# A decoder layer with convolution, retention and experts: another order at the start, products of ones, and small work moved between engines

## The reference

```python
z = rmsnorm(x, norm1_g) @ w_in                   # 1024 x 3072
a, b, q, k, v, g = split(z)                      # six parts of 512 columns
u = a * sigmoid(b)                               # convolution group: depthwise, 31 taps
c = silu(layernorm(causal_depthwise_conv(u)))
q, k = rope(q), rope(k)                          # retention group: 4 heads of 128
o, state = retention(q, k, v)                    # chunks of 128 tokens, one after the other
o = silu(g) * group_norm(o)                      # norm of each head
x = x + concat(c, o) @ w_out
x = x + moe(rmsnorm(x, norm2_g))                 # 32 experts, 2 for each token, 1024 x 256
x = x + rmsnorm(p @ w_ple) * sigmoid(x @ w_ple_gate)
y = rmsnorm(x, final_norm_g)                     # the states are outputs too
```

## Time and profile before

| what | value |
| --- | --- |
| median of 3 runs | 738.96 us (735.79 to 739.05) |
| profiled execution | 741.15 us, span 739.4 us |
| mean granted TensorE clock | 0.97 |
| TensorE, VectorE, ScalarE, GpSimd busy | 685.8, 557.8, 405.3, 331.6 us |
| opening and convolution, to the first retention scores | about 0 to 176 us |
| retention and output projection | about 176 to 302 us |
| routing | about 302 to 337 us |
| experts | about 337 to 659 us |
| last stage | about 659 to 739 us |

### The profile page before, as it was taken

The page is one execution under the profiler, slowest core; times in us unless marked ns, Lnnn a source line. Parts: engine busy times, 40 slices in busy tenths (PEclk is TensorE's granted clock), DMA queues, the critical chain, the costliest instruction groups (busy, mean ns, idle before and its releaser), DMA issues.

```text
span 739.4 us, 13518 instructions
## 1 busy us (share of the span) xinstructions
PE 685.8 (93%) x5000; PEld 637.9 (86%) x5000; DVE 557.8 (75%) x818; ACT 405.3 (55%) x538; POOL 331.6 (45%) x238
## 2 busy tenths in 40 slices
PE   5999999889999999977999999999999999957995
PEld 3899999888989889737988999999999998847995
DVE  4599999946662443676898888998888888948763
ACT  5431322325451132654787888888888888852322
POOL 3031499993466220014366656666666665110101
PEclk9999999989999999896999999999999999996998
DMA  9531431310038282703788999999999999685211
GB/s 272 187 127 34 139 103 58 110 63 11 1 126 262 72 257 87 297 1 141 282 300 319 344 342 342 359 356 362 386 369 370 373 363 351 216 287 192 72 58 58
DMA packets 54383, 156.15 MB, mean 211 GB/s; under 512 B 8842, under 2 KB 34634, under 8 KB 41275
## 3 DMA queue, kind: packets, MB, share of 16 engines
q1 hardware_dynamic: 38676, 133.77, 50.4%
q10 hardware_dynamic: 9519, 12.32, 5.0%
q0 software_dynamic: 6144, 9.45, 3.7%
HBM read 149.82 MB, written 17.59 MB: 226 GB/s over the span
## 4 chain that ended last, share of the span: by engine, by line
PE 66%; POOL 11%; DVE 8%; DMA 6%; issue 4%; ACT 3%; SPq 0%; POOLq 0%; ACTq 0%; DVEq 0%
PE bank L549 60%; PE bank L553 6%; POOL ring_parts L2054 4%; DVE ring_parts L1301 2%; POOL qTx L2067 2%; POOL Sm L2066 2%; DMA catT<-in_x_prompt 2%; DMA out<-front 1%; DMA ring<-in_w_expert_up 1%; POOL z L2069 1%; POOL z L2068 1%; ACT down_high L1921 1%; DMA uext<-expert_rows 1%; DVE hT_high L1432 1%; DVE ring_parts L1453 1%
## 5 line engine op out<-in xcount | busy, mean ns | idle before, releaser
L549 PE MATMUL bank<-ring_parts,hT_high 128*128 128x256 f32 x1344 | 190.5, 286 | 2.1 <-POOL ring_parts L2054 2.1
L549 PEld LDWEIGHTS bank<-ring_parts,hT_high 128*128 128x128 f32 x1344 | 174.8, 194 | 2.3 <-POOL ring_parts L2054 2.3
L549 PE MATMUL bank<-catT_parts,hT_high 128*128 128x256 f32 x1056 | 148.3, 289 | 4.5 <-DVE hT_high L1432 2.9
L1301 DVE TENSOR_TENSOR ring_parts<-ring,catT_parts 128x2048 fp32r<-128x2048 f32 x64 | 146.4, 2287 | 7.1 <-ACT catT_parts L1829 6.8
L549 PEld LDWEIGHTS bank<-catT_parts,hT_high 128*128 128x128 f32 x1056 | 134.4, 193 | 6.6 <-DVE hT_high L1432 4.0
L1829 ACT ACTIVATE catT_parts<-ring 128x2048 fp32r<-128x2048 f32 x64 | 122.5, 1915 | 23.0 <-PE bank L549 18.8
L2054 POOL TENSOR_TENSOR ring_parts<-ring,ring_parts 128x2048 fp32r<-128x2048 f32 x14 | 64.4, 4600 | 64.1 <-ACT ring_parts L1653 63.7
L1453 DVE TENSOR_TENSOR ring_parts<-ring,down_high 128x2048 fp32r<-128x2048 f32 x31 | 71.1, 2292 | 28.0 <-ACT down_high L1921 28.0
L1158 DVE SCALAR_TENSOR_TENSOR bank<-uext,cpar,bank 128x512 f32<-128x512 f32 x116 | 86.7, 748 | 0.0
L2200 POOL DMA_INDIRECT expert_rows<-front,cur_code x32 | 34.2, 1067 | 93.1 <-issue 89.7
L549 PE MATMUL bank<-down_high,cv_parts 128*128 128x512 f32 x248 | 65.3, 405 | 0.0
(11 more groups left out here) (298 smaller groups left out, 1156.4 us busy)
## 6 DMA issues: line engine op xcount, KB each, us to landing
ring<-in_w_expert_gate SPq DMA_DIRECT2D x32, 1024.0 KB, 6.8
ring<-in_w_expert_up SPq DMA_DIRECT2D x32, 1024.0 KB, 7.1
ring<-in_w_expert_down SPq DMA_DIRECT2D x32, 1024.0 KB, 7.1
ring<-in_w_in SPq DMA_DIRECT2D x12, 1024.0 KB, 7.2
ring<-in_w_out SPq DMA_DIRECT2D x4, 1024.0 KB, 5.0
ring<-in_w_ple_gate SPq DMA_DIRECT2D x4, 1024.0 KB, 10.3
catT<-in_x_prompt SPq DMA_DIRECT2D x4, 512.0 KB, 8.2
z<-in_x_prompt SPq DMA_DIRECT2D x4, 512.0 KB, 6.8
```

The lines of the kernel that those rows point to most:

```text
L549: return nc.tensor.matmul(out, lhsT, rhs, start=start, stop=stop, skip_group_check=True)
L1301: V.tensor_tensor(ring_r[:, 3 * par + m, :], ring[:, 3 * par + m, :], cat_r[:, m * CHUNK:(m + 1) * CHUNK].bitcast(F32), ALU.subtract).then ...
```

## The change

- **Opening.** SyncE issues x tiles 0, 1, 2, then the first weight block, then 3 and 4. TensorE runs 6 products of ones (bf16, 256 columns, into bank 3, read by nobody) before it waits for the norm's weights and 20 behind the two long products; VectorE sets `counters` to 1.0 for that. Three transposes come first, then passes 0 and 1 of the first half with tiles 3 and 4 between, then passes 0 and 1 of the second half, and the third passes last. Low part 0 is made half on VectorE and half on GpSimd, which first waits for all five normalisations.
- **Sample copies.** Four copies on GpSimd become one on ScalarE, behind z block 6.
- **Low part 9** starts one rotation earlier in GpSimd's queue. **Low part 12** goes to VectorE, ahead of tile 3's statistics. `k_decay(4)` goes behind the gate of tile 3.
- **Variance sum.** It goes from ahead of the first scores to behind z block 10 of tile 1, in banks 7 and 6, and the wait for the roots into `retention_out(0)`.
- **Gate values, overflow list** go behind the expert steps; `ple_norm(4)` behind a step of the last loop, `ple_norm` 0 to 3 into the last stage, ahead of each tile's `x3`. The tiles they use are moved to other buffers.

```diff
-                for i in ((0, 1), (2, 3, 4), (), ())[s]:
+                for i in ((0, 1, 2), (3, 4), (), ())[s]:
...
+            def idle_products(n, b):
+
+                for _ in range(n):
+                    mm(bank[b][:, 0:2 * P], counters[:, 0, :], counters[:, :, :].rearrange("p a n -> p (a n)"), True, True)
+
+            pe.wait_ge(S["zeroed"], 9)
+            idle_products(6, 3)
             pe.wait_ge(S["gbc_in"], 16)
             for a in range(2):
                 mm(bank[4 + a][:, :], Sm[0:1, 0, :], gbc[0:1, a * 512:(a + 1) * 512], True, True).then_inc(g_ps, 1)
+            idle_products(20, 3)
             pe.wait_ge(S["ident_in"], 16)
-            x_T_first(0)
-            x_T_first(1)
-            conv_in(0, 0, 0, (0,))
-            x_T_first(2)
-            conv_in(0, 0, 0, (1,))
-            x_T_first(3)
-            conv_in(0, 0, 0, (2,))
-            x_T_first(4)
-            conv_in(0, 0, 1)
+            for i in range(3):
+                x_T_first(i)
+            for which in range(2):
+                conv_in(0, 0, 0, (which,))
+                x_T_first(3 + which)
+            conv_in(0, 0, 1, (0, 1))
+            for half in range(2):
+                conv_in(0, 0, half, (2,))
...
-            pe.wait_ge(S["tail_u"], CT)
+            pe.wait_ge(S["tail_u"], 1)
...
                 pe.wait_ge(S["kz_done"], i + 1)
+                if i == 0:
+                    pe.wait_ge(S["cstd"], 2)
...
-                    pe.wait_ge(S["csum"], 2)
                     pe.wait_ge(S["tail_sb"], 2)
-                    channel_sum(squares[:, 0, :], 5, S["var_done"])
-                    pe.wait_ge(S["cstd"], 2)
                 retention_scores(i)
                 if i < TT - 1:
                     z_part(10, i + 1)
+                    if i == 0:
+                        pe.wait_ge(S["csum"], 2)
+                        channel_sum(squares[:, 0, :], 7, S["var_done"])
                     retention_out(i)
...
+            def w_low_first(c):
+
+                dve.wait_ge(S["w_hi"], c + 1)
+                n = CHUNK // 2 if c == 0 else CHUNK
+                V.tensor_tensor(ring_r[:, c, 0:n], ring[:, c, 0:n], ring_r[:, 4 + c, 0:n].bitcast(F32),
                                 ALU.subtract).then_inc(S["w_lo"], 1)
...
+                if i == TT - 2:
+                    dve.wait_ge(S["w_hi"], 13)
+                    V.tensor_tensor(ring_r[:, 0, :], ring[:, 0, :], ring_r[:, 4, :].bitcast(F32),
+                                    ALU.subtract).then_inc(S["w_lo"], 1)
...
-            ple_rstd()
             for q in range(1, NX):
                 step(0, q)
-                ple_norm(q - 1)
...
                 step(LOOPS - 1, q, last=q == NX - 1)
-                if q < 2:
-                    ple_norm(NX - 1 + q)
+                if q == 0:
+                    ple_rstd()
+                    ple_norm(TT - 1)
+                if q == 2:
+                    pick_gates()
+            overflow_info()
...
+                else:
+                    ple_norm(ORDER[n])
+                    dve.wait_ge(S["ple_sb"], n + 1)
                 for part in range(len(columns(n))):
                     x3(n, part)
...
+                if c == 6:
+                    act.wait_ge(S["u_done"], 3 * CT)
+                    A.activation(kTs[:, :, 0:NS].rearrange("p c (b t) -> p c b t", b=NB), sext[:, :, :, HIST:HIST + NL],
+                                 ACT.Copy).then_inc(S["tail_u"], 1)
...
-                for i in range(3):
+                for i in range(3 - j):
                     rotate(j, i)
                 w_low(7 + 2 * j)
-                rotate(j, 3)
+                for i in range(3 - j, TT - 1):
+                    rotate(j, i)
...
-                if i == TT - 2:
-                    w_low(12)
```

More of the change, by code:

```diff
@@ L243, in build @@
         gmx, m1, m2 = (work(TT) for _ in range(3))
-        gsum, e2, t1 = (kept(TT) for _ in range(3))
-        gexp = kept(TT * NG).rearrange("p (i n) -> p i n", i=TT)
+        late = flat_u[:, CHUNK:CHUNK + 3 * TT + TT * NG + 2 * NE]
+        gsum, e2, t1 = (late[:, n * TT:(n + 1) * TT] for n in range(3))
+        gexp = late[:, 3 * TT:3 * TT + TT * NG].rearrange("p (i n) -> p i n", i=TT)
         gval = work(TT * NG).rearrange("p (i n) -> p i n", i=TT)
@@ L257, in build @@
         ov = kept(NE)
-        ovi = kept(NE)
-        ovb = kept(NE)
+        ovi, ovb = (late[:, 3 * TT + TT * NG + n * NE:3 * TT + TT * NG + (n + 1) * NE] for n in range(2))
         ovw = kept(NE)
@@ L614, in conv_in @@
                         m = mm(out, w, (h_lo if x_part else h_hi)[:, k, lo:hi], which == 0 and k == 0, which == 2 and k == KT - 1)
-                if half:
+                if half and 2 in passes:
                     m.then_inc(S["ab_done"], 1)
-            pe.wait_ge(S["zeroed"], 8)
+            def idle_products(n, b):
[3 more added lines that the diff above has]
+            idle_products(6, 3)
             pe.wait_ge(S["gbc_in"], 16)
@@ L1098, in h_low @@
                 m.then_inc(S["hlo_sb"], 1)
-            def w_low_second():
-                dve.wait_ge(S["w_hi"], 2)
-                dve.wait_ge(S["w_lo"], 1)
-                V.tensor_tensor(ring_r[:, 1, :], ring[:, 1, :], ring_r[:, 5, :].bitcast(F32),
+            def w_low_first(c):
+                dve.wait_ge(S["w_hi"], c + 1)
+                n = CHUNK // 2 if c == 0 else CHUNK
+                V.tensor_tensor(ring_r[:, c, 0:n], ring[:, c, 0:n], ring_r[:, 4 + c, 0:n].bitcast(F32),
                                 ALU.subtract).then_inc(S["w_lo"], 1)
-            x_norm(0)
-            x_norm(1)
+            for i in range(3):
+                x_norm(i)
             h_low(0)
-            x_norm(2)
             h_low(1)
@@ L1469, in _ @@
             x_low(0, 0)
-            jj = bc(C("ovj", 1), 2, NE)
-            then(V.tensor_tensor(ovt[0:1, 0, :, :], bc(ovb[0:1, :], 1, NOV), jj, ALU.is_le))
-            then(V.tensor_tensor(ovt[0:1, 1, :, :], bc(ovi[0:1, :], 1, NOV), jj, ALU.is_le))
-            then(V.tensor_tensor(ovt[0:1, 0, :, :], ovt[0:1, 0, :, :], ovt[0:1, 1, :, :], ALU.subtract))
-            then(V.tensor_tensor(ovt[0:1, 0, :, :], ovt[0:1, 0, :, :], bc(C("expert", 1), 1, NOV), ALU.mult))
-            then(V.tensor_reduce(ovf[0:1, 0:NOV], ovt[0:1, 0, :, :], AX.X, ALU.add))
@@ L1477, in _ @@
-            then(V.tensor_copy(ovf[0:1, NOV:NOV + 1], ovi[0:1, NE - 1:NE]))
-            V.tensor_copy(ovinfo[:, 0:NOV + 1], ovf[0:1, :]).then_inc(S["idx_done"], 1)
-            dve.wait_ge(S["gexp_done"], 2)
-            then(V.tensor_reduce(gsum, gexp, AX.X, ALU.add))
-            then(V.tensor_scalar(t1, e2, 1.0, None, ALU.add))
-            then(V.tensor_tensor(t1, t1, gsum, ALU.mult))
-            then(V.reciprocal(gates[:, :, 0], t1))
-            then(V.tensor_tensor(gates[:, :, 1], gates[:, :, 0], e2, ALU.mult))
@@ L1486, in _, with pick_gates @@
             dve.wait_ge(S["ple_sq"], 2 * TT)
             V.tensor_tensor(rst3[:, :], ssq3[:, :, 0], ssq3[:, :, 1], ALU.add).then_inc(S["ple_var"], 1)
+            def pick_gates():
+                dve.wait_ge(S["gexp_done"], 2)
+                then(V.tensor_reduce(gsum, gexp, AX.X, ALU.add))
+                then(V.tensor_scalar(t1, e2, 1.0, None, ALU.add))
+                then(V.tensor_tensor(t1, t1, gsum, ALU.mult))
+                then(V.reciprocal(gates[:, :, 0], t1))
+                then(V.tensor_tensor(gates[:, :, 1], gates[:, :, 0], e2, ALU.mult))
@@ new lines, in overflow_info @@
+            def overflow_info():
+                jj = bc(C("ovj", 1), 2, NE)
+                then(V.tensor_tensor(ovt[0:1, 0, :, :], bc(ovb[0:1, :], 1, NOV), jj, ALU.is_le))
+                then(V.tensor_tensor(ovt[0:1, 1, :, :], bc(ovi[0:1, :], 1, NOV), jj, ALU.is_le))
+                then(V.tensor_tensor(ovt[0:1, 0, :, :], ovt[0:1, 0, :, :], ovt[0:1, 1, :, :], ALU.subtract))
+                then(V.tensor_tensor(ovt[0:1, 0, :, :], ovt[0:1, 0, :, :], bc(C("expert", 1), 1, NOV), ALU.mult))
+                then(V.tensor_reduce(ovf[0:1, 0:NOV], ovt[0:1, 0, :, :], AX.X, ALU.add))
+                then(V.tensor_copy(ovf[0:1, NOV:NOV + 1], ovi[0:1, NE - 1:NE]))
+                V.tensor_copy(ovinfo[:, 0:NOV + 1], ovf[0:1, :]).then_inc(S["idx_done"], 1)
@@ L2079, in _ @@
             G.tensor_copy(ring_r[:, 4, :], ring[:, 0, :]).then_inc(S["w_hi"], 1)
-            for c in (0, *range(2, 7)):
+            pool.wait_ge(S["w_hi"], 1)
+            pool.wait_ge(S["xn_done"], TT)
+            n = CHUNK // 2
+            G.tensor_tensor(ring_r[:, 0, n:], ring[:, 0, n:], ring_r[:, 4, n:].bitcast(F32),
+                            ALU.subtract).then_inc(S["w_lo_rest"], 1)
+            for c in range(2, 7):
                 w_low(c)
@@ L2092, in _ @@
                 w_low(8 + 2 * j)
-            pool.wait_ge(S["u_done"], 3 * CT)
-            for c in range(CT):
-                G.tensor_copy(kTs[:, c, 0:NS].rearrange("p (b t) -> p b t", b=NB),
```

(2 more changed lines are left out.)

28 lines of the change are left out of this document (17 added, 11 removed).

## The result

| what | before | after |
| --- | --- | --- |
| median | 737.82 us (20 runs, 735.04 to 739.49) | 733.30 us (20 runs, 729.54 to 735.55) |
| ratio of the times | 1 | 0.9937, 95% interval 0.9925 to 0.9949 |
| profiled execution | 741.15 us, span 739.4 | 734.08 us, span 732.3 |

The change gains 4.5 us, 0.6%, against a forecast of 4.3. The two profiled executions differ by 7.1 us, since the one of before lies 3.3 above its median and the one of after 0.8; what is read off the pair alone says 2.5 us too much. First the page's first part, after; it answers to the earlier trace rows.

A forecast was written before the change was run, and what follows sets the result against it. TensorE, busy 93% of the span, was taken as the bound through its waits and slow stretches. Opening 2.8, middle -1.3, low part 12 0.3 and loop 2.5 sum to 4.3 us: 734.7 from a 738.96 median, range 728.5 to 738.8.

The forecast's parts named there:

- Opening: Start of the kernel: convolution rows' transposes start at 29.8 or 31.3 instead of 33.4; gain 2.8 us, bounds 2.1 and 3.6.
- (B): Rival, opening: products of ones hold the clock through the transposes; opening gains 3.6, sum 5.1, 733.9 us; chance 0.12.
- weight block's slip to 13.5: Opening: the first weight block, cast from 11.27 on, slips to about 13.5 behind the third x tile's 0.5 MB.
- at the same rate: Opening: assumption that 2.5 MB in place of 2 load at an unchanged rate, putting the weight block at about 13.5.
- Middle: Low part 9, sample copies, variance sum: 0.3 us gained, 1.6 lost to a slow stretch; -1.3, bounds +3.7 and -2.5.
- half-speed stretch: Middle, at 190 us, behind PE's wait of some 3.7 us: one new stretch at half clock, charged at 1.6 us.
- Low part 12 and key decay: Ahead of the gated heads: the key decay leaves the chain; gain 0.3 us, bounds 0 and 1.57.
- Loop: Expert loop: PE's waits for the tokens' low part fall from 2.9 us to 0.4; gain 2.5, bounds 1.5 and 2.9.
- Last stage: Four normalisations of 1.28 us join VectorE's cycle, which at 12.2 fits PE's period of 12.25; cost 0, without cover 5.1.
- (D): Rival, last stage: the normalisations are exposed on VectorE; fully exposed they cost 5.1 us, 739.8; chance 0.10.
- (A): Rival, middle: PE's saving of 3.7 us passes on, second tile's scores not held by the reciprocal; sum 9.3, 729.7; chance 0.18.
- (C): Rival, opening and middle: gains die out, opening 2.1, middle -2.5, sum 2.4 us, 736.6; chance 0.30.

The follow-up runs named there:

- e7: e2 without the 26 products of ones; 729.52 us, ratio 0.9893 to the kernel before.
- e2: The changed kernel with the variance sum put ahead of the first tile's scores again; 729.16 us, ratio 0.9886 to the kernel before.
- e9: e6 with weight block 11's low part on VectorE too; 726.48 us, ratio 0.9849 to the kernel before.
- e11: The changed kernel with low part 12 back on GpSimd and the third key decay back in its place; 732.45 us, ratio 0.9926 to the kernel before.
- e1: The changed kernel without its 26 products of ones; 734.48 us, ratio 0.9947 to the kernel before.
- e5: The kernel before with only the middle changed (low part 9 earlier, sample copies on ScalarE, variance sum later); 737.48 us, ratio 1.0002.
- e8: The changed kernel with its x tiles loaded in the order of the kernel before; 735.55 us, ratio 0.9980 to the kernel before.
- e10: The changed kernel without its middle (rotations, sample copies and variance sum as before); 732.68 us, ratio 0.9933 to the kernel before.
- e4: The kernel before with only the change's expert loop and last stage; 735.57 us, ratio 0.9970.
- e3: The kernel before with only the change's opening; 733.95 us, ratio 0.9937.
- e6: e2 with weight block 10's low part moved from GpSimd to VectorE; 731.03 us, ratio 0.9918 to the kernel before.
- e12: e9 with the first tile's z part ahead of the variance sum and VectorE's convolution scaling later; 726.41 us, ratio 0.9852 to the kernel before.

## Why the prediction was right, by its own steps

The gain came out at 4.5 us against 4.3. The time itself, 734.7, is 1.4 above the measured 733.30, since it started from a median of three runs that lies 1.1 above the one of twenty.

**Opening, 2.8, bounds 2.1 and 3.6.** Its rows came out: squares near 9, no normalisation of 3.2 us, rows' transposes between the bounds of 29.8 and 31.3 or slightly before. The pair of profiles gives 3.9. Over all executions it is 32.79 (33.34, 32.40, 32.62) less 29.85 (the eight above): 2.9. The size was right. By the prediction the 1.5 us between the bounds hang on the clock; with the products of ones it is 1.1, since both cases occur, five executions at full clock with the rows at 29.2 to 29.6 and three at half with 30.5 to 30.7. A sign of (B), 8 transposes in 1.16 us near 17, stood in the trace, but its mechanism, that the products of ones hold the clock, is refuted: e7 has the full clock without them, e2, e9 and e11 lose it with them. What decides between the two cases stays open. Part 4 of the Trainium skill's "TensorE: Matmul & The Clock Gate", by which transposes don't count as activity, doesn't fit e1: from the end of the long products at 6.2 to 15.3 PE had nothing but transposes, 16 at 0.23 us each and then, from 14.43, 8 at 0.14, so the clock rose behind transposes alone. The weight block's slip to 13.5 did not come: its cast starts at 10.1 to 11.7 in the ten executions with the new order of the loads and at 10.2 to 11.3 in the four with the old. The step that failed is "at the same rate": from 5 to 8 us the DMA moved 267 to 299 GB/s with the old order (268 before) and 340 to 381 with the new (381 in the change). Why the old order has that dip is not shown.

**Middle, -1.3, bounds +3.7 and -2.5.** Right in place, mechanism and size: PE's second-tile retention resumed 0.36 us earlier relative to the opening (190.14 - 185.86 - 3.92; predicted 0.3), behind a wait of 3.38 (predicted 3.7), at a clock of 0.50. e2 shows that the variance sum's place is the cause: with it first, the wait is 0.61. The half-speed stretch, priced at 1.6, is not a constant: from the retention's start to the next z block PE took 4.01 us before, 6.76 after (2.75 more), 5.60 in e5 (1.59 more). In e8 the same wait of 3.39 was followed by full clock. The middle's loss of 1.2 on average (e10) is the forecast's, spread by this; that the average of five lies within 0.1 of it is in part luck.

**Low part 12 and key decay, 0.3, lower bound 0.** It was 0 (e11). The power step starts at 216.43 in the change and at 216.44 in e11, as the prediction itself argued. The 0.3 was the key decay's, and it wasn't in the way: in e11 it ends at 218.8, and the gate's product behind it starts at 219.31 for want of VectorE's normalised heads.

**Loop, 2.5, bounds 1.5 and 2.9.** The waits for the tokens' low part fell from 2.9 to 0.9 us (predicted 0.5). e4's median says 2.4. From the end of an early PE wait for VectorE in the loop (347.52 before) to the end of the one for ScalarE behind it (655.02 before) the traces say more: 307.50, 306.26 and 307.39 in the kernels with the old loop, 302.7 to 304.7 in the eleven with the new one, mean 303.6, so 3.4 us; of these 0.5 come back between that wait and the last stage's first transposes, 14.8 and 15.3 us on average. That is 2.9: by the traces the term was 0.4 too small, by the times it was right. The wait that the prediction names gives 2.0 of it; what else in the loop got shorter no run here separates.

**Last stage, 0.** From its first transposes to the end: 739.4 - 669.79 = 69.6 before, 68.5 and 68.4 in e3 and e5, 68.8 after. (D) is refuted.

**Sum.** 2.9 - 1.2 + 0 + 2.9 + 0 = 4.6 by the traces, 4.5 by the medians, 4.3 forecast. Left out is the stretch from the gated heads to the loop's early wait, 124.4 us on average in the three executions with the old loop and 123.6 in the eleven with the new one, from 122.6 to 124.8; with so wide a spread the 0.8 can't be called a gain, and the sum is good to about 1 us. (A) is refuted by the wait of 3.38; (C) had the middle at -2.5, near where the profiled execution was (188.99 - 191.30 = -2.3), and the opening at 2.1, where it was not. Measured alone the parts make 6.5; the four intervals together leave some 2.4 us either way, so that they don't add up is not shown.

## What to carry to other kernels

A wait removed ahead of a chain on another engine only brings TensorE to that chain earlier: find the chain (here the deviation, reciprocal, scaling, statistics, second tile's scores), and put first what starts it, even at the price of a short wait there. e2 did this, and e9, built on it, is 11.4 us under the kernel before, where the change is 4.5. A low part on GpSimd is waited for itself and also holds a VectorE addition (4.32 us in place of 0.76). Moving it to VectorE took away the first wait (2.24 us) and not the second: VectorE, now with the subtraction in its own queue, was no earlier (2.35 against 2.04). After each such move the next engine's queue has to be read again (e6, e12).

## What the hardware showed beyond this

- The kernel before and the changed one each spread over 4 to 6 us in 20 runs, and the spread follows the mean granted clock: of the change's 20 runs the five fastest (729.54 to 731.72) had 0.978 to 0.98, the five slowest (734.58 to 735.55) 0.967 to 0.971. Part of it lies between the gated heads and the loop's early wait. Before took 125.2 us for it, e3 124.0 and e5 124.1, whose code there is the same, at clocks of 0.93, 0.94 and 0.96; e1 took 124.8 and e6 122.6, again with the same code there, at 0.95 and 0.97. Set against the sum of 4.6, the pair of profiles has 1.9 us more for this stretch, 1.0 more for the opening (3.9), 0.8 more for the last stage, 1.1 less for the middle (-2.3) and 0.1 less for the loop: together the 2.5 us by which it overstates the change. Why one execution's clock falls behind a wait of 3.39 us and another's doesn't (e5, e8) stays open.
- In the first 20 us the granted clock reads 1.00 in the kernel before while its transposes go at the pace of 1.2 GHz (8 in 1.97 us); there the pace has to be read from durations.
